# First mixer: attention scores and values two heads at a time, twelve projections beside them, and the recurrence's scores in alternating column halves

## The reference

```
h = rmsnorm(x, norm_mix);  proj = h @ w_in          # q, k, v | hq, forget f/b, hi, hg | two gates
y_att = softmax(q k^T / 8) v  @ w_up_att            # 8 heads of 64, 2 key/value heads, 512 x 512 scores
y_hg  = hgrn2_bidirectional(hq, f, b, hi, hg) @ w_up_hg   # 4 heads of 128, chunks of 64 tokens
x = x + (sigmoid(gate0) * y_att + sigmoid(gate1) * y_hg) @ w_out
mod = silu(c) @ ada_w + ada_b                       # 96 rows of the second block's modulation
```

## Time and profile before

| | us |
|---|---|
| median of 3 runs (3462.25 to 3465.48) | 3463.79 |
| the profiled execution | 3464.62 |
| its span, first to last instruction | 3462.9 |

### The profile page before, as it was taken

The page is one execution under the profiler, slowest core; times in us unless marked ns, Lnnn a source line. Parts: engine busy times, 40 slices in busy tenths (PEclk is TensorE's granted clock), DMA queues, the critical chain, the costliest instruction groups (busy, mean ns, idle before and its releaser), DMA issues. The chain is left out here.

```text
span 3462.9 us, 30884 instructions
## 1 busy us (share of the span) xinstructions
PE 3122.9 (90%) x11312; PEld 1749.2 (51%) x11312; DVE 2067.9 (60%) x4458; ACT 740.3 (21%) x1638; POOL 663.8 (19%) x649
## 2 busy tenths in 40 slices
PE   8999799988989877878887889999999988999998
PEld 3453454443333333333333334536864467878887
DVE  5555742577767767776776417535667777456433
ACT  2133211222222222222222220112111133121000
POOL 0110100244444444444444100000000000000000
PEclk9999899999999999998989899999999999999999
DMA  5743412599999999999999522112235554212222
GB/s 195 249 149 125 158 49 73 238 421 421 421 421 422 419 418 421 414 421 414 416 415 421 244 90 98 61 37 100 73 129 212 213 208 179 80 61 87 92 86 78
DMA packets 118680, 799.23 MB, mean 231 GB/s; under 512 B 13728, under 2 KB 16416, under 8 KB 31872
## 3 DMA queue, kind: packets, MB, share of 16 engines
q0 software_dynamic: 91312, 619.09, 44.4%
q1 hardware_dynamic: 27216, 178.15, 14.4%
HBM read 767.83 MB, written 29.36 MB: 230 GB/s over the span
## 5 line engine op out<-in xcount | busy, mean ns | idle before, releaser
L1315 PE MATMUL po<-pair,diag 128*128 128x512 f32 x2048 | 991.6, 641 | 198.8 <-ACT diag L1398 198.6
L1492 DVE SCALAR_TENSOR_TENSOR pair<-pair,h_tm 128x1024 f32<-128x1024 f32 x512 | 619.0, 1225 | 322.4 <-DMA pair<-in_peer_uv,idx 316.2
L1315 PEld LDWEIGHTS po<-pair,diag 128*128 128x128 f32 x2048 | 411.5, 205 | 751.8 <-issue 487.3
L1208 POOL DMA_INDIRECT pair<-in_peer_uv,idx x512 | 591.3, 1155 | 933.4 <-PE po L1315 656.1
L1391 ACT ACTIVATE ge<-a 128x2 f32<-128x2 f32 (+2 forms) x178 | 36.4, 204 | 928.1 <-DVE pair L1492 928.1
L1914 PE MATMUL acc<-a,ring 128*128 128x512 f32 x512 | 220.9, 592 | 0.0
L1398 ACT ACTIVATE diag<-ident,wt 128x128 f32<-128x128 f32 x512 | 169.1, 392 | 40.8 <-DVE wt L1496 40.3
L1914 PEld LDWEIGHTS acc<-a,ring 128*128 128x128 f32 x512 | 97.3, 190 | 122.0 <-issue 122.0
L523 PE MATMUL acc<-hT,first 128*128 128x512 f32 x304 | 136.1, 602 | 5.4 <-ACT mg L707 5.4
L1625 PE MATMUL bank<-hT,ring 128*128 128x256 f32 x592 | 139.8, 379 | 0.0
L1625 PE MATMUL bank<-hT,weight_sums 128*128 128x256 f32 x592 | 139.8, 379 | 0.0
(11 more groups left out here) (492 smaller groups left out, 4129.3 us busy)
## 6 DMA issues: line engine op xcount, KB each, us to landing
ring<-in_w_fc SPq DMA_DIRECT2D x62, 1024.0 KB, 4.9
mg<-in_ada_w POOLq DMA_DIRECT2D x96, 512.0 KB, 4.9
tab<-s_tables SPq DMA_DIRECT2D x16, 1664.0 KB, 6.4
ring<-in_w SPq DMA_DIRECT2D x15, 1024.0 KB, 4.9
first<-in_w_first SPq DMA_DIRECT2D x14, 1024.0 KB, 5.4
other<-in_w_first SPq DMA_DIRECT2D x14, 1024.0 KB, 4.9
s_tables<-weight_sums POOLq DMA_DIRECT2D x8, 1664.0 KB, 6.5
s_tables<-table POOLq DMA_DIRECT2D x8, 1664.0 KB, 6.1
```

The lines of the kernel that those rows point to most:

```text
L1208: pool.indirect_dma_start(out=pair[:, at, :], out_offset=None, in_=core.dram["peer_uv"][:, :], in_offset=bass.IndirectOffsetOnAxis(ap=idx[ ...
L1315: last = pe.matmul(po[:, t % 2, half * 512:(half + 1) * 512], diag[:, at, :], pair[:, at, D + half * 512:D + (half + 1) * 512], start=firs ...
L1492: dve.scalar_tensor_tensor(row, row, 1.0, h_tm[:, t, :], ALU.mult, ALU.mult, accum_out=a[:, s:s + 1]).then_inc(dotted, 1)
```

## The change

Seven edits in `first_mixer`, no operation of attention, recurrence or modulation added or taken away:

1. Units in pairs. Unit u is now head pair u // 8, head u % 2, block u // 2 % 4 (`place`). PE works 16 steps i with two score matmuls one behind the other, for a = 0 and a = 1, in two banks, after one wait for both exponentials of the step before.
2. `mix(j)` makes both heads of a pair in one go, the column halves alternating matmul by matmul: 4 times 8 matmuls in place of 8 times 4. The two copies out follow together.
3. Twelve jobs beside attention (`beside`): in steps 1, 2, 3, 5, 6, 7, 9, and so on, none in every fourth step. 4 HV, 4 G and 4 GATE0; a further GATE0 job stands ahead of the last `mix`.
4. `modulate(1 + u % 2)`: 48 rows beside attention in place of 32. The recurrence keeps 12: 4, 4 in head 0, 4 in head 1.
5. The recurrence's score matmuls go through the chunks of both column halves in turns.
6. Fillers: GATE0's last three, then 5 jobs in head 0, 5 in head 1, 3 in head 2 and 3 in head 3. Before: three, then 6, 6, 6 and 2.
7. ACT takes GATE0's sixth job ahead of the exponentials of head 0, not behind them; the sigmoid of GATE0 stands behind the first `keys_out`; `up` has new places in DVE's list.

```
-            for u in range(32):
-                j, a, t = u // 8, u // 4 % 2, u % 4
-                if u >= 2:
-                    pe.wait_ge(expd, u - 1)
-                pe.matmul(bank[:, u % 2, :], qk[64 * a:64 * a + 64, 1 + j, t * P:(t + 1) * P], qk[64 * a:64 * a + 64, 0, :], ...)
-                if u % 4 == 2:
-                    job(JOB_HV + u // 4)
-                if u >= 3:
-                    transposes(u - 3)
-                if u >= 7 and u % 4 == 3:
-                    mix(u // 4 - 1)
+            for i in range(16):
+                if i:
+                    pe.wait_ge(expd, 2 * i)
+                for u in (2 * i, 2 * i + 1):
+                    j, a, t = place(u)
+                    pe.matmul(bank[:, u % 2, :], qk[64 * a:64 * a + 64, 1 + j, t * P:(t + 1) * P], qk[64 * a:64 * a + 64, 0, :], ...)
+                if beside(i) is not None:
+                    job(beside(i))
+                if i >= 5 and i % 4 == 1:
+                    mix(i // 4 - 1)
+                if i:
+                    transposes(2 * i - 2)
+                    transposes(2 * i - 1)
...
             def mix(j):
+                pe.wait_ge(copied, 8 * j + 8)
+                if j:
+                    pe.wait_ge(out_done, 2 * j)
                 for b in range(TT):
+                    for a in range(2):
+                        last = pe.matmul(bank[64 * a:64 * a + 64, 4 + a, :], v[:, b, 64 * a:64 * a + 64], probT[:, b, a, :], ...)
...
-                    for c in range(NCH):
+                    for n_ in range(NCH // 2 * NBL * 2):
+                        c, i = n_ // (2 * NBL) * 2 + n_ % 2, n_ // 2 % NBL
...
-                modulate(1)
+                modulate(1 + u % 2)
...
             for h in range(GH):
+                mask(h)
+                if h < 2:
+                    up(ups.pop(0))
                 if h + 1 < GH:
                     gates_one(h + 1)
+                if h < 2:
+                    up(ups.pop(0))
                 states(h, 0, 4)
+                if h < 2:
+                    modulate(4)
+                    up(ups.pop(0))
                 states(h, 4, NCH - 1)
```

More of the change, by code:

```diff
@@ L482, in _, with place, beside @@
                 pool.dma_start(ada[:, m % 4, :], w[m // 2 * P:(m // 2 + 1) * P, m % 2 * D:(m % 2 + 1) * D]).then_inc(ada_landed[m % 4], 16)
+        def place(u):
+            return u // 8, u % 2, u // 2 % 4
+        def beside(i):
+            return JOB_HV + i - i // 4 - 1 if i % 4 else None
         def rows(d, i):
@@ L571, in transposes, with mix @@
                 last.then_inc(transposed, 1)
[L573 to L577, removed]
+            def mix(j):
+                pe.wait_ge(copied, 8 * j + 8)
+                if j:
+                    pe.wait_ge(out_done, 2 * j)
                 for b in range(TT):
-                    last = pe.matmul(bank[64 * a:64 * a + 64, 4 + a, :], v[:, b, 64 * a:64 * a + 64], probT[:, b, a, :],
-                                     start=(b == 0), stop=(b == TT - 1))
+                    for a in range(2):
+                        last = pe.matmul(bank[64 * a:64 * a + 64, 4 + a, :], v[:, b, 64 * a:64 * a + 64], probT[:, b, a, :],
+                                         start=(b == 0), stop=(b == TT - 1))
                 last.then_inc(mixed, 1)
@@ L618, in score @@
                 for d in range(2):
-                    for c in range(NCH):
+                    for n_ in range(NCH // 2 * NBL * 2):
+                        c, i = n_ // (2 * NBL) * 2 + n_ % 2, n_ // 2 % NBL
                         r_ = GC * (c % 2)
[L621 to L624, removed]
+                        last = pe.matmul(pa[r_:r_ + GC, d, c // 2, GB * i:GB * (i + 1)], kk[:, d, c, i, :],
+                                         qd[:, d, c * GC + GB * i:c * GC + GB * (i + 1)], start=True, stop=True,
+                                         skip_group_check=True)
                 last.then_inc(a_scores, 1)
@@ L665, in out_sum @@
                 pe.matmul(pn, ones[:, :], sqh, start=True, stop=True).then_inc(o_summed, 1)
-            fill = list(range(JOB_GATE0 + 1, JOB_UH))
+            fill = list(range(JOB_GATE0 + 5, JOB_UH))
             def filler(count):
@@ L676, in _ @@
                 turn_keys(h)
-                filler(1)
+                filler(1 if h < 2 else 0)
                 score(h)
@@ L771, in _ @@
                                scale=AD ** -0.5, accum_out=stat[:, 1, u % 8:u % 8 + 1]).then_inc(expd, 1)
-                if u % 4 == 2:
-                    take_later(JOB_HV + u // 4)
-                if u >= 3:
+                i = u // 2
+                if u % 2 and beside(i) is not None:
+                    take_later(beside(i))
+                if u % 2 and i:
                     copy(u - 3)
[L776 to L779, removed]
+                    copy(u - 2)
+                if u % 2 and i >= 6 and i % 4 == 2:
+                    out(i // 4 * 2 - 2)
+                    out(i // 4 * 2 - 1)
             copy(30)
             copy(31)
+            take_later(JOB_GATE0 + 4)
             out(6)
@@ L820, in invert_out @@
                 act.activation(rstd, rstd, ACT.Exp, scale=-0.5).then_inc(o_rooted, 1)
-            later = list(range(JOB_GATE0 + 1, JOB_UA)) + list(range(JOB_UA, JOB_UH))
+            later = list(range(JOB_UA, JOB_UH))
             def filler(count):
@@ L828, in filler @@
                     x = later.pop(0)
[L829 to L835, removed]
+                    if x >= JOB_GATE1:
                         if x == JOB_GATE1:
@@ L1081, in _ @@
                     up(ups.pop(0))
[L1082 to L1086, removed]
+            assert not rows_left
             assert not ups
```

61 lines of the change are left out of this document (25 added, 36 removed).

## The result

| | before | changed |
|---|---|---|
| median (us), 4 runs each | 3463.02 (3458.55 to 3465.48) | 3442.40 (3439.18 to 3446.41) |
| profiled execution | 3464.62 | 3439.18 |
| its span | 3462.9 | 3437.3 |
| first scores to first UH job | 375.8 | 352.0 |

The ratio is 0.9938 (95% interval 0.9925 to 0.995): 20.6 us less, forecast 31, inside the range and nearer its upper end. In the profiled executions the stretch that the change touches is 23.8 us shorter. The first scores started 0.5 us later, and what follows the first UH job took 2928.0 us in place of 2930.3. The ten experiments, in which that part is the same code, show 2925 to 2931 there, so these 2 us are not shown to be an effect. The profiled execution of the changed kernel is the fastest of its four: the two profiles lie 25.4 us apart, the medians 20.6.

The account below looks back on a forecast made before the run. PE was taken to set the pace, with holes. Attention's end at 315.3 plus recurrence 175.7 plus low clock 9.7 put the first UH job at 500.7, before 532.6: gain 31.9, called 31, so 3433 us, range 3421 to 3450.

Parts of the forecast that it names:

- PE's work: Attention and recurrence: PE saves 34.3 us in attention and 2.4 in the recurrence, 36.7 together.
- Values: Attention: two heads' values on alternating column halves take 3.58 us in place of 7.16, saving 14.3 in all.
- The scores: Attention: two scores on different row halves take 1.06 us a pair, 16 pairs 17.0 in place of 33.6, saving 16.6.
- Recurrence's scores: Recurrence: score matmuls alternating column halves save 0.6 us a head, bounds 0 and 2.2.
- Twice the rate: Two array halves, rows or columns, overlap in full; read from 128-wide rows and assumed for streams of 512.
- Holes of the attention: PE waits 7.5 us behind the first scores, 10.2 in steps 4, 8 and 12 together, 0.6 at the last transposes.
- The 16 rows of modulation: Rows added beside attention cost nothing there, since they lie under 9.0 us of PE work a step.
- Holes of the recurrence: PE waits 24.7 us: first keys 3.1, states 5.4, 5.5, 4.6, 1.1, UA5's bank 1.0, roots 0.8, last norm 3.2.
- low clock: Half-clock work behind holes: 9.7 us in the sum, besides 2.3 behind the attention's first wait.
- part overlap: Rival: halves overlap only partly in 512-wide streams; about 3445 us midway, about 3439 by the skill's rule; chance 0.08.
- The longer chain: Rival: late rows hold DVE's maxima, 1.5 us more in each of 16 attention steps; about 3445 to 3455; chance 0.08.
- The slow rival: Clock stays low over recurrence heads 0 and 1; 3477 us, chance 0.03; sign: 0.5 for over two thirds of 340 to 420.

Follow-up runs that it names:

- values apart: Changed kernel with whole-array work (four transposes, a job in the last pair) between the values of a pair's two heads: 3460.01 us, ratio to before 0.9979.
- one half: Changed kernel with units paired within one head, so both score matmuls of a step use the same 64 rows: 3456.49 us, ratio to before 0.998.
- holes filled: Changed kernel with 38 idle matmuls, whose results nothing uses, put in PE's holes: 3421.79 us, ratio to before 0.9876.

## Why the prediction was right, and where its sizes were off

- **PE's work.** Foretold 36.7 us less, measured 35.0. Values 14.3 (values apart: 14.9). The scores saved the 16.6 foretold, but not by overlap alone: 13.6 are overlap (one half: 13.7), 3.0 come of two scores standing in one piece, since a pair in one half takes 1.91 from start to start where two single ones took 2.10. Recurrence's scores 0.6 a head (4.54 to 3.91). "Twice the rate" for 512-wide streams, taken from rows of 128, is shown. The Trainium skill's table ("TensorE: Matmul & The Clock Gate", "Why this matters for your kernels") has 3.07 times for four row tiles and 2.38 for three column tiles; two halves by that would give about 1.6, an estimate. The trace does not agree: it shows 2.0 for rows (1.13 for two against 1.12 for one) and for columns (3.65 against 7.2 with the heads apart).
- **Holes of the attention.** Foretold 7.5, 10.2 and 0.6; measured 7.4, 3 times 3.06 and 0.4. The 16 rows of modulation cost nothing there, as the experiment that puts them back confirms.
- **Holes of the recurrence.** Foretold 3.1, 5.4, 5.5, 4.6, 1.1, 1.0, 0.8 and 3.2, together 24.7; measured 3.5, 3.9, 5.6, 4.4, 1.2, 0, 0 and 3.0, 21.6. In head 0 the hole is 1.5 shorter; PE had lost 3.3 us at half clock ahead of it, which fits, but no run parts the two.
- **The term that was mis-sized is low clock.** The prediction put "9.7" to it besides 2.3 behind the first wait, 12.0 in all, by one wait's price of 2.4 with 1 absorbed and 2.5 for the three holes of the attention. It measured 22.7. Each of those holes was 0.97 and 2.09 us with four transposes between, and each set 3.4 us of work to half clock (0.66 in the window from 201 to 206): 1.7 apiece, 5.1. Behind the hole ahead of the first keys 1.6 went; behind the two for states in heads 0 and 1 4.6 and 3.7, behind the one in head 2 3.4. Filling the holes gave 18.4 us of the total back, so that waiting costs clock is shown: 38.6 us of holes went with 22.7 of low clock. Why the stretches behind the waits of heads 0 and 1 are longer than the one behind 5.4 us before is open.
- **One stretch stands behind no hole.** The prices above and 2.6 behind the first scores leave 1.7 us of the 22.7. They lie in the stretch from 355.3 to 358.7, for which the sum had no term at all. PE had worked for 10 us without a hole, 6.8 of them at clock 1.00, and the clock fell right behind the last of the recurrence's score matmuls. Nine stretches in eight of the twelve profiles begin so, 0.2 to 0.4 us after the start of a score group's last matmul, one of them in the kernel with its holes filled (424.5 us, the only one it has left; a pause of 1.0 us stands ahead of that group's last matmul). In the kernel before, whose scores go in the old order, none of four groups has one. Whether it is these matmuls or the waits that in the other eight lie 8 to 10 us earlier is open, and so is whether edit 5, which saved 0.6 a head, pays for itself; no run puts the old order back.
- **Forecast 3433, measured 3442.4.** The 8 us by which the profile missed 31.9 are work 1.7 too much, low clock 10.7 too little, holes 4.3 too many. The holes set off part of the error in the clock, which is luck. The rest of the difference to the median is the spread of the runs, the profiled one being the fastest.
- **The rivals.** By its time alone the result would fit the rival of part overlap (about 3445) better than the forecast of 3433; only the groups of 1.13 and 3.65 us in the trace rule it out. The longer chain falls with the step of 5.43 us and with 0.4 us in all for which DVE waited for a row beside attention. Its price was also wrong as it stands: 1.5 us more is hidden whole by a slack of 2.8 in the 12 steps with a job, so 6 us are left, about 3439. The slow rival named the right quantity, but low clock ended each time within 10 us of work: from 340 to 420 us the granted clock was 0.83 in the mean, at the low level for a third of the time and not for the two thirds that would have shown it.

## What to carry to other kernels

Matmuls that use 64 rows or 64 columns of the array ran two at a time here when neighbours in the list used different halves: order the loop so that the halves alternate. The scores wrote two banks, as did the values; row halves in one bank were not tried. When PE's list gets shorter, count the holes one by one, also those of 2 to 3 us, and price the low clock behind each: in the changed kernel single holes of 3 to 6 us cost from half of their own length to a little more than all of it again. In the kernel before one of 3.17 us cost nothing, so this is a price and not a law. Work moved into them, even one step of the same loop, is worth more than the time it covers. Background work on a second engine belongs where that engine waits, and never ahead of what the first engine needs next.

## What the runs showed of the hardware that was not expected

- PE reached two matmuls down its list, so its list is not started strictly in order, as the text ahead of the prediction has it for every engine: values of two column halves that stand one after the other took 5.42 us, alternating 3.65, with whole-array work between them 7.2.
- Three holes of 0.97 and 2.09 us with 0.66 us of transposes between them lowered the granted clock every time, in each of the six profiles that had them. With both scores in one half the first of the two is gone, and 2.09 us alone did it, three times of three. In the kernel before a hole of 3.17 us did not:

```profile
407.04 1.16 PE L650 MATMUL bank<-work,hv 128*128 128x128 f32 x8 [3.17 <-DVE work L1008]
```

- Matmuls without a use, 0.43 us a record in 30 us of holes, kept the clock at 0.99 to 1.00 and made the program 18 us faster.
